# Output tiles that take the sample rows' bank first, row statistics in two groups, and one of the last residual passes on ScalarE and GpSimd

## What is computed

```python
def merge(x, m_out, m_gate, a_out, a_gate, c_out, c_gate, w_out, g_post):
    mix = jnp.concatenate([m_out * jax.nn.silu(m_gate), a_out * jax.nn.silu(a_gate),
                           c_out * jax.nn.silu(c_gate)], axis=-1)
    return x + rms_norm(mix @ w_out, g_post)
```

## Time and profile before

| | us |
|---|---|
| median of three runs | 1937.49 |
| span of the profiled execution (first to last instruction) | 1933.6 |
| the four output tiles on TensorE | 1704.8 to 1911.2 |
| from the last matmul to the first residual pass | 1911.2 to 1917.6 |
| the five residual passes | 1917.6 to 1929.0 |
| from the last pass to the end | 1929.0 to 1933.6 |

### The profile page before, as it was taken

One profiled execution on the slowest core, in us unless ns is written; L12 is line 12 of the kernel. 1 busy time (PEld: TensorE's weight loads), 2 busy tenths in 40 slices (PEclk: granted clock), 3 DMA queues, 4 the chain that ended last, 5 costly groups with the idle time before them and its releaser, 6 DMA issues.

```text
span 1933.6 us, 21312 instructions
## 1 busy us (share of the span) xinstructions
PE 1723.5 (89%) x7943; PEld 1280.0 (66%) x7943; DVE 803.1 (42%) x1315; ACT 575.6 (30%) x911; POOL 678.0 (35%) x448
## 2 busy tenths in 40 slices
PE   5899999999999769999989999996558788799995
PEld 3677775457789657777668878885234455577774
DVE  4300010008998976675662144202465455511113
ACT  5412223322222133322412321314144443222221
POOL 2555531112333226675544544341000000023331
PEclk9999999999999979999999999998758878889998
DMA  6444531213334337677534634337413333442222
GB/s 229 142 125 134 156 111 33 66 36 92 110 89 133 116 98 245 202 216 239 173 109 133 203 108 146 119 112 259 103 55 114 103 99 104 156 175 87 81 81 103
DMA packets 139141, 251.11 MB, mean 130 GB/s; under 512 B 25681, under 2 KB 62518, under 8 KB 135506
## 3 DMA queue, kind: packets, MB, share of 16 engines
q10 hardware_dynamic: 66864, 122.84, 20.2%
q1 hardware_dynamic: 55450, 74.86, 12.0%
q0 software_dynamic: 16736, 52.18, 9.4%
HBM read 206.19 MB, written 43.66 MB: 129 GB/s over the span
## 4 chain that ended last, share of the span: by engine, by line
PE 74%; DVE 13%; DMA 4%; ACT 4%; issue 2%; ACTq 1%; SPq 1%; POOL 1%; DVEq 0%; POOLq 0%
PE acc L387 16%; PE acc L389 15%; PE acc L388 15%; PE acc L382 4%; PE acc L383 4%; PE ps_c L914 3%; PE ps_b L649 2%; DMA arena<-z_prompt 2%; PE ps_c L657 2%; PE acc L1645 1%; DVE arena L1592 1%; PE ps_c L2039 1%; PE acc L2034 1%; PE ps_a L1078 1%; PE ps_a L1147 1%
## 5 line engine op out<-in xcount | busy, mean ns | idle before, releaser
L345 POOL TENSOR_TENSOR w_lo<-w_raw,w_hi 128x1024 fp32r<-128x1024 f32 (+1 forms) x200 | 471.6, 2358 | 867.5 <-ACT w_hi L341 867.3
L387 PE MATMUL acc<-w_hi,x_hi 128*128 128x512 f32 (+1 forms) x1472 | 581.9, 395 | 7.9 <-DVE keep L848 5.3
L389 PE MATMUL acc<-w_hi,x_lo 128*128 128x512 f32 (+1 forms) x1472 | 566.3, 385 | 0.0
L388 PE MATMUL acc<-w_lo,x_hi 128*128 128x512 f32 (+1 forms) x1472 | 565.3, 384 | 0.0
L341 ACT CAST w_hi<-w_raw 128x1024 fp32r<-128x1024 f32 (+1 forms) x200 | 204.2, 1021 | 763.3 <-PE acc L383 712.7
L387 PEld LDWEIGHTS acc<-w_hi,x_hi 128*128 128x128 f32 x1472 | 279.0, 190 | 105.4 <-issue 42.0
L389 PEld LDWEIGHTS acc<-w_hi,x_lo 128*128 128x128 f32 x1472 | 278.1, 189 | 55.6
L388 PEld LDWEIGHTS acc<-w_lo,x_hi 128*128 128x128 f32 x1472 | 279.1, 190 | 51.0 <-issue 0.5
L382 PE MATMUL acc<-w_hi,x_hi 128*64 128x512 f32 (+1 forms) x368 | 141.2, 385 | 0.0
L383 PE MATMUL acc<-w_lo,x_hi 128*64 128x512 f32 (+1 forms) x368 | 140.9, 384 | 0.0
L2154 DVE TENSOR_TENSOR arena<-arena (+1 forms) x16 | 14.0, 888 | 176.6 <-ACT arena L417 176.6
(11 more groups left out here) (429 smaller groups left out, 2016.1 us busy)
## 6 DMA issues: line engine op xcount, KB each, us to landing
w_raw<-in_w_in ACTq DMA_DIRECT2D x136, 512.0 KB, 3.7
z_prompt<-z_tile ACTq DMA_DIRECT2D x68, 256.0 KB, 2.6
w_raw<-in_w_out ACTq DMA_DIRECT2D x32, 512.0 KB, 3.6
arena<-z_prompt SPq DMA_DIRECT2D x4, 2088.0 KB, 10.2
w_raw<-in_w_mem_kv ACTq DMA_DIRECT2D x16, 512.0 KB, 3.6
arena<-q_sample POOLq DMA_DIRECT2D x32, 256.0 KB
arena<-z_prompt SPq DMA_DIRECT2D x10, 512.0 KB, 7.3
between<-z_prompt SPq DMA_DIRECT2D x10, 512.0 KB, 10.0
```

Source lines behind the costliest of these rows:

```text
L345: nc.gpsimd.tensor_tensor(out=w_lo[:, c % 2, :, 0:w], in0=w_raw[:, c % RAWS, :, 0:w], in1=w_hi[:, c % 2, :, 0:w].bitcast(F32), op=ALU.subt ...
L387: nc.tensor.matmul(acc[m][:, 0:w], xh, wh, start=first, stop=False)
L388: nc.tensor.matmul(acc[m][:, 0:w], xh, wl, start=False, stop=False)
L389: last = nc.tensor.matmul(acc[m][:, 0:w], xl, wh, start=False, stop=end)
```

## The change

In an output tile, TensorE and ScalarE take the sample bank first and then the banks 0 to 3 (`bank_order`); `p` is the place in that order, `m` the bank, and the semaphores count by `p`. VectorE works on the sample rows of a tile first and multiplies the four prompt banks by `g_post` behind that. After the last tile the statistics are made twice: for the sample rows alone, and then for the four prompt groups. VectorE makes four residual passes, in the order sample, 0, 1, 2. Group 3 is scaled by ScalarE (a copy with a factor for each row) and its input row is added by GpSimd (`gpsimd_y`). SyncE stores in the order sample, 0, 1, 2, 3.

```diff
+        def bank_order(kind):
+            if kind == "mem":
+                return range(NU_MEM)
+            return (MT, *range(MT)) if kind == "y" else range(MT + 1)
+
...
-                for m in range(nm):
+                for p, m in enumerate(bank_order(kind)):
                     if c == 0 and not (isinstance(n, int) and n == 0):
...
-                        if m < back:
-                            pe.wait_ge(acc_read, before - back + m + 1)
+                        if isinstance(n, int) and n == N_Y0:
+                            pe.wait_ge(acc_read, before)
+                        elif p < back:
+                            pe.wait_ge(acc_read, before - back + p + 1)
...
-                    if m == nm - 1:
+                    if p == nm - 1:
                         last.then_inc(chunk_used, 1)
-                    if c == CH - 1 and m < nm - 1:
+                    if c == CH - 1 and p < nm - 1:
                         last.then_inc(acc_ready, 1)
...
-            for m in range(nm):
+            for p, m in enumerate(bank_order(kind)):
                 rows = P if m < MT else 2 * R
-                if m < nm - 1:
-                    act.wait_ge(acc_ready, acc_ready_base(n) + m + 1)
+                if p < nm - 1:
+                    act.wait_ge(acc_ready, acc_ready_base(n) + p + 1)
                 else:
                     act.wait_ge(chunk_used, CH * n + CH)
...
+        y_turn = (MT, *(m for m in range(MT) if m != MT - 1))
+
         def sync_y_out(sp):
-            for m in range(MT + 1):
+            for m in (*y_turn, Y_POOL):
                 n, _, y = y_place(m)
-                sp.wait_ge(y_ready, m + 1)
+                if m == Y_POOL:
+                    sp.wait_ge(y_last, 1)
+                else:
+                    sp.wait_ge(y_ready, y_turn.index(m) + 1)
                 sp.dma_start(y, y_t[0:n, m, :]).then_inc(y_out, 16)
...
         def scalar_y(act):
-            act.wait_ge(y_var, 1)
-            nc.scalar.activation(y_root, y_st, ACT.Sqrt).then_inc(y_std, 1)
+            for i, ms in enumerate((slice(MT, MT + 1), slice(0, MT))):
+                act.wait_ge(y_var, i + 1)
+                nc.scalar.activation(y_root[:, ms], y_st[:, ms], ACT.Sqrt).then_inc(y_std, 1)
+            act.wait_ge(*at("y_scaled"))
+            nc.scalar.activation(y_t[:, Y_POOL, :], y_t[:, Y_POOL, :], ACT.Copy, scale=y_inv[:, Y_POOL:Y_POOL + 1]).then_inc(y_std, 1)
+
+        def gpsimd_y(pool):
+            pool.wait_ge(y_std, 3)
+            pool.wait_ge(res_in, 16 * (MT + 1))
+            nc.gpsimd.tensor_tensor(out=y_t[:, Y_POOL, :], in0=y_t[:, Y_POOL, :], in1=x_res[Y_POOL], op=ALU.add).then_inc(y_last, 1)
...
-                for m in range(MT):
-                    dve.wait_ge(acc_read, acc_base(n) + m + 1)
-                    nc.vector.tensor_tensor(out=y_t[:, m, cols], in0=y_t[:, m, cols], in1=g_post[:, cols], op=ALU.mult)
-                dve.wait_ge(acc_read, acc_base(n) + MT + 1)
+                dve.wait_ge(acc_read, acc_base(n) + 1)
...
                 dve.wait_ge(y_part, 4 * (n - N_Y0) + 4)
+                for m in range(MT):
+                    dve.wait_ge(acc_read, acc_base(n) + m + 2)
+                    nc.vector.tensor_tensor(out=y_t[:, m, cols], in0=y_t[:, m, cols], in1=g_post[:, cols], op=ALU.mult)
             tile_loop(dve, N_Y0, N_END, body)
-            dlink(nc.vector.tensor_reduce(out=y_st, in_=y_sum, axis=AX.X, op=ALU.add))
-            nc.vector.tensor_scalar(y_st, y_st, 1.0 / D, RMS_EPS, ALU.mult, ALU.add).then_inc(y_var, 1)
-            dve.wait_ge(y_std, 1)
-            rsqrt_refined(y_st, y_root, y_inv)
+            for i, ms in enumerate((slice(MT, MT + 1), slice(0, MT))):
+                dlink(nc.vector.tensor_reduce(out=y_st[:, ms], in_=y_sum[:, ms, :], axis=AX.X, op=ALU.add))
+                nc.vector.tensor_scalar(y_st[:, ms], y_st[:, ms], 1.0 / D, RMS_EPS, ALU.mult, ALU.add).then_inc(y_var, 1)
+                dve.wait_ge(y_std, i + 1)
+                rsqrt_refined(y_st[:, ms], y_root[:, ms], y_inv[:, ms])
+            nc.vector.drain().then_inc(reached("y_scaled"), 1)
             dve.wait_ge(res_in, 16 * (MT + 1))
-            for m in range(MT + 1):
+            for m in y_turn:
                 n = y_place(m)[0]
                 nc.vector.scalar_tensor_tensor(out=y_t[0:n, m, :], in0=y_t[0:n, m, :], scalar=y_inv[0:n, m:m + 1],
                                                in1=x_res[m][0:n, :], op0=ALU.mult, op1=ALU.add).then_inc(y_ready, 1)
...
             tile_loop(pool, N_Y0, N_END, lambda n: gpsimd_tile(pool, n))
+            gpsimd_y(pool)
```

More of the change, by code:

```diff
@@ L120, in hybrid_decoder_step @@
                         "qs_ready", "ifs_ready", "g_abs", "g_rows", "cmax", "ps_ready", "mixed_c",
-                        "sm_ready", "scv_ready", "ks_scaled", "bc_copied", "qspr_ready", "pws_ready",
+                        "sm_ready", "scv_ready", "ks_scaled", "bc_copied", "qspr_ready", "pws_ready", "y_scaled",
                         ),
@@ L389, in tensor_tile @@
                             last = nc.tensor.matmul(acc[m][:, 0:w], xl, wh, start=False, stop=end)
-                    if m == nm - 1:
+                    if p == nm - 1:
                         last.then_inc(chunk_used, 1)
-                    if c == CH - 1 and m < nm - 1:
+                    if c == CH - 1 and p < nm - 1:
                         last.then_inc(acc_ready, 1)
-                    if m == nm - 1:
+                    if p == nm - 1:
                         next(steps[1], None)
-                    if m == (nm - 1) // 2 or m == nm - 1 or (often and m == 0):
+                    if p == (nm - 1) // 2 or p == nm - 1 or (often and p == 0):
                         next(steps[0], None)
@@ L413, in scalar_evacuate @@
                     if m < MT:
-                        act.wait_ge(acc_read, acc_base(n) + m)
+                        act.wait_ge(acc_read, acc_base(n) + p)
                         nc.scalar.activation(z_tile[:, 0, :], acc[m][:, :], ACT.Square,
@@ L782, in hybrid_decoder_step @@
         qbc_in = [sem(f"qbc_in{i}") for i in range(GS)]
-        (row_scored, new_in, probs_s) = (
-            sem(n) for n in ("row_scored", "new_in", "probs_s"))
+        (row_scored, new_in) = (
+            sem(n) for n in ("row_scored", "new_in"))
         (row_summed, mix_stored) = (
@@ L2105, in hybrid_decoder_step @@
             sem(n) for n in ("gp_in", "res_in", "y_part", "y_var", "y_std", "y_ready", "y_out"))
+        y_last = sem("y_last")
+        Y_POOL = MT - 1
         def sync_y_early(sp):
```

## The result

The changed kernel takes 1943.22 us (median of 8 runs, 1938.98 to 1947.09) against 1937.64 for the kernel before: a ratio of 1.0028, 95% interval 1.0016 to 1.0040, or 3.1 to 7.8 us more. It is slower.

The account below looks back on a forecast made before the run. The tail was taken as bound by the stores as much as by VectorE. With GpSimd first, 1925.70 + 3.9 + 3 x 2.53 = 1937.2, end 1937.6, +4.0 on 1937.49: 1941.5 us, range 1937.9 to 1942.6.

Parts of the forecast that it names:

- Bank order at no cost on the path: Output tiles: same 28 matmuls a chunk, same end; GpSimd's cover of 1.43 us at tile ends keeps about 0.9.
- Bank 3 last, 1.73 behind the last matmul: After the last chunk: VectorE multiplies bank 3 from 1912.55 to 1913.24, ending the loop there instead of at 1915.71.
- Two groups, first pass 5.86 behind the last matmul: Statistics: two groups run one behind the other, 1.5 us later; first pass at 1916.68, 0.91 us earlier than before.
- ScalarE 2.0, GpSimd 4.6: Group 3 in the tail: ScalarE's scaling takes 2.0 us, GpSimd's add over 2048 columns 4.6.
- GpSimd first, pass 0 about 6.8: Residual passes: GpSimd's add goes ahead of pass 0 and stretches it from 2.34 us; +4.0 us, chance 0.66 with its variant.
- Four landings 2.53 apart from a first store 14.88 behind the last matmul: Final stores: first 1 MB store issued at 1925.70, landing 3.9 later, three more 2.53 apart, end 1937.6.
- The range's 0.7 for a store that straggles: Final stores: allowance in the forecast range of up to 0.7 us for a late store.
- VectorE keeps its turn: Rival, residual passes: queued passes 0 to 2 go before GpSimd, last store lands alone; +1.0 us, 1938.5, chance 0.20.
- No contention: Rival, residual passes: VectorE's passes and GpSimd's add do not hinder each other; -0.4 us, 1937.1, chance 0.08.
- the term of 0.5 us for the runs' scatter: Whole time: allowance in the forecast range of about 0.5 us for scatter between runs.
- the 3.9 us between the profiled span and the median: Whole time: median 1937.49 against span 1933.6; the difference taken as outside the span and unchanged.
- the 0.2% that the prediction took as its line: Whole time: a measurement tells some 0.2%, 3.9 us, from no change; same 0.57, slower 0.40, faster 0.03.

Follow-up runs that it names:

- E1: Changed kernel with only the bank order kept: one group of statistics, five VectorE passes, sample last, nothing on ScalarE and GpSimd; 0.9975 of before.
- E8: Bank order and two groups of statistics, five VectorE passes with sample last, nothing on ScalarE and GpSimd; single run, tail 21.42 us.
- E2: Changed kernel without the share on ScalarE and GpSimd: five VectorE passes, sample first; 0.9998 of before, tail 22.51 us.
- E7: Changed kernel with GpSimd's add waiting for the last VectorE pass; single run, tail 26.75 us.
- E5: Changed kernel with VectorE's passes in four pieces, second input from PSUM accumulators instead of SBUF residual rows; single run, tail 23.69 us.
- E6: Changed kernel with GpSimd's add also waiting for the end of the sample pass; single run, tail 26.7 us.
- E4: Changed kernel with stores in the order sample, 3, 0, 1, 2; 1.0010 of before, tail 24.75 us.
- E9: The changed kernel as it is, compared with the kernel before a second time; ratio 1.0030, tail 26.95 us.

## Why the prediction was right and wrong

The mechanism of the tail was right in each part, and the tail was forecast at 26.8 us (1937.6 less 1910.82) and measured at 26.9. That it came so close is partly luck: the first prompt store was issued 0.4 us earlier than forecast, and the four landings took 0.5 us longer. The four parts of the change, one behind the other, are the differences of tails: the order -2.7 (E1 against before), the two groups +1.4 (E8 against E1), the sample pass in front +1.1 (E2 against E8), the share on ScalarE and GpSimd +4.4 (the change against E2). They sum to +4.2.

- *Bank order at no cost on the path*: right. From the first output matmul to the last take 205.3, 205.6 and 205.3 us in the kernel before and 205.8 and 205.5 in the changed one; no chunk came late.
- *Bank 3 last, 1.73 behind the last matmul*: 1915.60 - 1913.87 = 1.73.
- *Two groups, first pass 5.86 behind the last matmul*: 5.56. The 0.20 behind the loop, taken over from the earlier trace rows, belonged to the sample chain's last wait there, and stands behind line 2184 now (0.23); behind the multiplication of bank 3 the reduction follows at once. VectorE's drain in front of the passes, for which no row was at hand, takes about 0.1: without it the first pass starts at 5.45 (E8).
- *ScalarE 2.0, GpSimd 4.6*: 2.00, and 4.49 alone (E7), 4.52 beside passes that don't contend (E5).
- *GpSimd first, pass 0 about 6.8*: 6.61, with GpSimd asking 0.25 before pass 0 was issued. The rule of the issue order that the prediction cited from the Trainium skill (SBUF — State Buffer, "Who interferes with whom") agrees here and in E6.
- *Four landings 2.53 apart from a first store 14.88 behind the last matmul*: issued at 14.47; the landings come at 18.38, 20.84, 23.45 and 26.50, so the last is 3.05 behind the third and not 2.53. That is no stray packet of one run: in E2, E4, E5, E6 and E9, where a 1 MB store also is the last of several that queue up, it lands 3.1 to 3.2 behind the one ahead of it, while in the kernel before the fourth, with the small store queued behind it, lands 2.57 behind the third. The range's 0.7 for a store that straggles covered it; the sum had left it out.
- *VectorE keeps its turn*, the main rival: it fell in E6, where a waiting GpSimd went ahead of a pass that was queued. It was also mispriced. I gave an add at the end +1.0 us from the stores alone; E7 made that order, and it cost +4.0, since GpSimd's closing drain of 7.2 us then ends the span. The schedule that the prediction priced at 1938.5 is in its tail as slow as the one that it forecast.
- *No contention* fell with the first stretched pass.

What failed is the step from the tail to the time and its range: the term of 0.5 us for the runs' scatter was too small. I forecast +4.0 and 1941.5, with 1942.6 as the upper end; the medians came out 5.6 apart and the time at 1943.2. Of the 5.6 the tail holds 4.2; the other 1.4 are inside the interval of 3.1 to 7.8, and whether any of them belongs to the change stays open. The 0.5 was read from three runs within 2.1 us of each other; eight runs of the changed kernel lie within 8.1, the medians of the kernel before in the three comparisons were 1937.6, 1939.2 and 1937.1, and three profiles of that one kernel have the first output matmul 7.8 us apart. The upper end was not even the sum of its own allowances: 0.15, 0.7 and 0.5 over 1941.5 give 1942.85, still under the 1943.2. I also took the 3.9 us between the profiled span and the median as lying outside the span. In every run for which both numbers are on record it is 1.6 or 1.7 (1942.5 and 1940.8; 1938.9 and 1937.2): the first profile was of a fast execution, and 2.2 of the 3.9 were scatter inside the span. That doesn't change a difference of tails, but it was the sign that the runs move by more than the 0.5. The change came out slower by 0.28%. That is over the 0.2% that the prediction took as its line, the side to which I had given 0.40, against 0.57 for the one below; the interval, from 0.16% on, reaches across the line.

## What to carry to other kernels

Work moved from VectorE to GpSimd ran beside VectorE only where VectorE's instructions had at most one input in SBUF (E5); with two it cost VectorE nearly its whole length, and an add of 2048 columns took GpSimd 4.49 us against 2.33 for VectorE's whole pass. At the end of a kernel ask what the stores wait for before making the compute shorter: here a small pass ahead of the large ones cost 1.1 us and a ready store queued last 2.2, while the pass taken from VectorE saved nothing. And compare tails, or other stretches that an edit touches, between profiles before reading a difference of spans: here the stretches that it doesn't touch moved by more than the edit was worth.

## What was not expected of the hardware

GpSimd's closing drain ends 7.2 us behind its last computation, in every profile: subtraction to 1902.0 and drain from 1899.7 for 9.5 us in the kernel before, add to 1929.8 and drain to 1937.0 in E7. E7, whose last step is on GpSimd, ended about 2.7 us later for it than its last landing at 23.59 and the 0.4 us that the change has behind its last landing would give. A 1 MB store that was the last of several queued up landed about 3.1 us behind the one ahead of it instead of 2.5; why, no run here shows. And one program, the kernel before, had the stretch in front of its output tiles 7.8 us longer or shorter, with the granted clock between 0.78 and 0.80 over 410 us.
